# Moving the ada_w chunk loads of FFN1 from SyncE's DMA queue to GpSimd's

## What is computed

```python
m_lat = (jax.nn.silu(c) @ ada_w[l] + ada_b[l]).reshape(b, N_MOD, 1, d)
m_ctx = (jax.nn.silu(c_ctx)[None, :] @ ada_w[l] + ada_b[l]).reshape(1, N_MOD, 1, d)
x = x + 0.5 * m_lat[:, 2] * swiglu(modulate(rms_norm(x, norm1_g[l]), m_lat[:, 0], m_lat[:, 1]),
                                   ffn1_w_in[l], ffn1_w_out[l])
...
hx = modulate(rms_norm(x, norm2_g[l]), m_lat[:, 3], m_lat[:, 4])
```

## Time and profile before

| | us |
|---|---|
| median of 3 runs | 3235.8 |
| lowest and highest run | 3230.8 and 3244.4 |
| span of the profiled execution (first to last instruction) | 3242.2 |
| VectorE busy | 1721.2 |
| ScalarE busy | 945.0 |
| GpSimd busy | 4.5 |

### The profile page before, as it was taken

How to read it: one execution, slowest core, us unless ns; L and a number is a source line. 1 busy time by engine, 2 the same in 40 slices (tenths; PEclk the granted TensorE clock), 3 DMA queues, 4 the chain that set the end, 5 groups by cost and what they waited for, 6 DMA issues and landing times.

```text
span 3242.2 us, 40985 instructions
## 1 busy us (share of the span) xinstructions
PE 2930.8 (90%) x16213; PEld 2527.8 (78%) x16213; DVE 1721.2 (53%) x1907; ACT 945.0 (29%) x928; POOL 4.5 (0%) x13
## 2 busy tenths in 40 slices
PE   4659999999898989999999699977999999999997
PEld 3437787787777777778888598755688999999997
DVE  5765565656565555553342832265356555555555
ACT  4552121211111111212122532134234333333333
POOL 0000000000000000000000000000000000000000
PEclk9989999999999999999999899978898999999998
DMA  6755454544665665652333263312144666666662
GB/s 246 277 194 172 139 174 115 177 136 137 194 195 170 193 204 176 222 149 91 102 92 99 64 181 104 91 39 65 52 134 139 181 181 181 181 181 180 180 179 95
DMA packets 529879, 491.42 MB, mean 152 GB/s; under 512 B 17698, under 2 KB 448152, under 8 KB 523032
## 3 DMA queue, kind: packets, MB, share of 16 engines
q1 hardware_dynamic: 529464, 489.00, 49.5%
q0 software_dynamic: 352, 1.58, 0.2%
HBM read 488.44 MB, written 2.10 MB: 151 GB/s over the span
## 4 chain that ended last, share of the span: by engine, by line
PE 74%; DVE 9%; DMA 8%; ACT 5%; issue 4%; SPq 0%; DVEq 0%; ACTq 0%
PE py L736 9%; PE py L737 9%; PE py L738 9%; DMA chunk<-in_ada_w 7%; PE pg L736 6%; PE pg L737 6%; PE pg L738 6%; PE pu L736 6%; PE pu L737 6%; PE pu L738 6%; ACT wh L449 4%; DVE accl L1271 2%; DVE wl L1103 2%; PE py L885 1%; PE py L886 1%
## 5 line engine op out<-in xcount | busy, mean ns | idle before, releaser
L1103 DVE TENSOR_TENSOR wl<-raw,wh 128x2048 fp32r<-128x2048 f32 x364 | 833.8, 2291 | 828.6 <-ACT wh L449 828.4
L449 ACT ACTIVATE wh<-raw 128x2048 fp32r<-128x2048 f32 x364 | 695.4, 1911 | 1333.6 <-PE py L738 633.3
L736 PE MATMUL py<-ah,wh 128*128 128x512 f32 (+1 forms) x1408 | 481.4, 342 | 31.6 <-DVE xc L1232 26.3
L736 PE MATMUL pg<-hh,wh 128*128 128x512 f32 (+1 forms) x1408 | 478.8, 340 | 10.8 <-DVE hl L1167 6.3
L737 PE MATMUL py<-al,wh 128*128 128x512 f32 (+1 forms) x1408 | 477.3, 339 | 0.0
L738 PE MATMUL py<-ah,wl 128*128 128x512 f32 (+1 forms) x1408 | 476.7, 339 | 0.0
L736 PE MATMUL pu<-hh,wh 128*128 128x512 f32 (+1 forms) x1408 | 476.3, 338 | 0.0
L737 PE MATMUL pg<-hl,wh 128*128 128x512 f32 (+1 forms) x1408 | 476.1, 338 | 0.0
L738 PE MATMUL pg<-hh,wl 128*128 128x512 f32 (+1 forms) x1408 | 476.0, 338 | 0.0
L737 PE MATMUL pu<-hl,wh 128*128 128x512 f32 (+1 forms) x1408 | 475.5, 338 | 0.0
L738 PE MATMUL pu<-hh,wl 128*128 128x512 f32 (+1 forms) x1408 | 474.9, 337 | 0.0
(11 more groups left out here) (272 smaller groups left out, 2838.6 us busy)
## 6 DMA issues: line engine op xcount, KB each, us to landing
raw<-in_ffn_w_in SPq DMA_DIRECT2D x176, 1024.0 KB
chunk<-in_ada_w SPq DMA_DIRECT2D x192, 512.0 KB, 4.3
raw<-in_ffn_w_out SPq DMA_DIRECT2D x88, 1024.0 KB
raw<-in_ada_w SPq DMA_DIRECT2D x48, 1024.0 KB
raw<-in_mix_w_in SPq DMA_DIRECT2D x30, 1024.0 KB
raw<-in_mix_w_out SPq DMA_DIRECT2D x16, 1024.0 KB
raw<-in_mla_w_uq SPq DMA_DIRECT2D x12, 256.0 KB
xnat<-in_x SPq DMA_DIRECT2D x2, 1024.0 KB, 16.3
```

Source lines behind the costliest of these rows:

```text
L449: nc.scalar.activation(wh[:, slot % 2, :], raw[:, slot, :], ACT.Copy).then_inc(wh_ready, 1)
L736: mm(out_ap, w[0], xh_ap, start=first, stop=False, skip_group_check=True)
L1103: tt(wl[:, slot % 2, :], raw[:, slot, :], wh[:, slot % 2, :].bitcast(F32), ALU.subtract).then_inc(wl_ready, 1)
```

## The change

The 192 chunk loads are taken out of SyncE's loops. GpSimd gets them in two loops of its own, with the same wait on `chunk_free` and the same increment of `chunk_loaded`, so the order of the chunks and the two buffers are as before. They are issued as the loads of GpSimd's DMA queue (q0, which the profile calls software_dynamic; SyncE's is q1, hardware_dynamic). What the other engines do is the same, instruction for instruction.

```diff
--- before.py
+++ after.py
@@ -310,12 +310,6 @@
                     dst = raw[:, slot, :].rearrange("p (t n) -> p t n", n=512)
                 sp.dma_start(dst, src).then_inc(raw_loaded[slot], 64)
 
-            def chunk_load(unit, t, count):
-
-
-                sp.wait_ge(chunk_free, count + 1)
-                sp.dma_start(chunk[:, t % 2, :], ada_w[0, t * P:(t + 1) * P, ds(unit * CH + 3 * D, CH)]).then_inc(chunk_loaded[t % 2], 16)
-
             for s in range(RAW):
                 sp.wait_ge(wl_ready, FFN1_0 - RAW + s + 1)
                 ffn_slab(ffn1_w_in, ffn1_w_out, 0, s, s)
@@ -331,19 +325,9 @@
             with sp.Fori(0, 4) as i:
                 for s in range(GSLABS):
                     ahead(i, s)
-                    if s < 8:
-                        for t in (2 * s, 2 * s + 1):
-                            chunk_load(i, t, i * KT + t)
-
             with sp.Fori(4, 8) as i:
                 for s in range(GSLABS):
                     ahead(i, s)
-                    if s < 4:
-                        for t in range(4 * s, 4 * s + 4):
-                            chunk_load(i * 2 - 4, t, (i - 4) * (2 * KT) + t + 4 * KT)
-                    elif 5 <= s < 9:
-                        for t in range(4 * s - 20, 4 * s - 16):
-                            chunk_load(i * 2 - 3, t, (i - 4) * (2 * KT) + t + 5 * KT)
             for s in range(GSLABS - RAW):
                 ahead(8, s)
             with sp.Fori(9, GROUPS) as i:
@@ -422,6 +406,17 @@
             nc.gpsimd.memset(csp[:].bitcast(F32).rearrange("p a b -> p (a b)"), 0.0).then_inc(consts_ready, 1)
             for f, w in enumerate((ret_decay_fwd, ret_decay_bwd)):
                 pool.dma_start(dec[:, f * HEADS:(f + 1) * HEADS], w.to_broadcast([P, HEADS])).then_inc(rope_loaded, 16)
+
+            def chunk_load(unit, t, count):
+                pool.wait_ge(chunk_free, count + 1)
+                pool.dma_start(chunk[:, t % 2, :], ada_w[0, t * P:(t + 1) * P, ds(unit * CH + 3 * D, CH)]).then_inc(chunk_loaded[t % 2], 16)
+
+            with pool.Fori(0, 4) as i:
+                for t in range(KT):
+                    chunk_load(i, t, i * KT + t)
+            with pool.Fori(0, 8) as i:
+                for t in range(KT):
+                    chunk_load(i + 4, t, i * KT + (4 * KT + t))
 
             pool.wait_ge(y_free, Y_OUT)
             pool.dma_start(ropes[:].rearrange("p a b -> p (a b)"), rope).then_inc(rope_loaded, 16)
```

## The result

The changed kernel takes 3282.3 us (median of 4 runs, 3269.5 to 3285.0), the kernel before 3237.3 beside it: the ratio is 1.013, with a 95% interval from 1.0104 to 1.0155. It is 45 us slower. Forecast were 3207 us, within 3186 to 3262. All 192 chunk loads moved to GpSimd's queue.

What follows compares the result with a forecast made beforehand. It took chunk-load waits in groups 4 to 7 as the bound, about 51 us. Savings of 2.9, 2.3 and 2.0 (clock) made 7.2 us a group, 29 in four, off the median 3235.8: 3207 us, range 3186 to 3262.

Steps and rivals of the forecast that it cites:

- What bounds the kernel: FFN1 groups 4 to 7 lose some 12.7 us each to late chunk loads, about 51 us in all.
- VectorE's two kinds of round: Chunk loads in groups 4 to 7 took 3.58 us to landing, or 6.65 us when queued behind a slab load.
- TensorE's two waits: Per group in groups 4 to 7: 9.25 us ahead of the transposes at slab 5, 6.86 us ahead of slab 9.
- The price of a GpSimd load: Per chunk round, 0.22+0.15 us more than on SyncE, plus 0.1 us for a register address (bounds 0 and 0.3).
- d: Time the early slab load adds to the landing of c2: taken as 0.5 us, bounds 0.2 and 1.4.
- c2: Third of a step's four chunks, issued when the first one's operation ends; forecast to land after 3.8 us plus d.
- c4: First chunk of the next step, issued after c2's operation; its 6.65 us round was to become near 3.8.
- the working of the first half: Wait ahead of slab 5: 3.7+4d plus 0.7 us, so 6.4 us where it was 9.3; 2.9 won a group.
- the second half: Wait ahead of slab 9: 2.6+3d plus 0.5 us, so 4.6 us where it was 6.9; 2.3 won a group.
- The clock: Shorter TensorE stalls in groups 4 to 7 raise the granted clock: up to 3.4 us a group, 2.0 taken.
- Rival B: c2 waits for the slab's rest instead of c4: 3220 to 3240 us, chance 0.25.
- Rival C: GpSimd's loads are held up while VectorE works, at c2: 3250 to 3277 us, chance 0.23.

Runs made afterwards that it cites:

- experiment 5: Kernel before with four chunk buffers in groups 4 to 7, not two: 3160.5 us with loads on SyncE, 3159.5 us with loads on GpSimd and early slabs.
- experiment 2: Kernel before, chunks still on SyncE, but in groups 4 to 7 each slab load goes out early, ahead of the step's third chunk load: 3282.1 us, ratio 1.0153.
- e11: e5 with SyncE's slab loads in groups 4 to 7 held until GpSimd has issued the step's fourth chunk load: 3260.9 us, ratio 1.0057.
- experiment 1: Slab loads of groups 4 to 7 cut to one sixteenth in both kernels: 3239.2 us with chunks on GpSimd, 3223.4 us with them on SyncE.
- e5: Changed kernel with GpSimd's two loops unrolled, so every address and wait is a constant: 3275.9 us, ratio 1.0131.
- e7: Changed kernel, but in groups 4 to 7 SyncE issues a slab load only when the step's third chunk has landed: 3271.8 us, ratio 1.0127.
- e8: e7 with GpSimd's loops unrolled, so all its addresses and waits are constants: 3274.4 us, ratio 1.0113.

## Why the prediction was wrong

**What bounds the kernel** held: the loss of groups 4 to 7, VectorE's two kinds of round, TensorE's two waits. Groups 0 to 3 and the part behind group 7 didn't change, as said. Only the bound on what better chunk loads can win, 51 us, was too low: experiment 5 won some 73. The bound took the early groups' 139.8 us as the floor, and without waits a group of the second stretch takes 132.5.

**The price of a GpSimd load** was near. Landing alone 3.8 was taken, 3.9 measured. From release to issue 0.39 was taken (0.29 and 0.1 for a register address), 0.63 measured. With that corrected alone the forecast would still have been a gain.

**The step that failed is the slab's**, d, what a slab adds to the landing of c2. I took 0.5 us with an upper bound of 1.4. Measured in the first half of group 4, c2's kind of round took 6.1, 7.2, 5.2 and 6.2 us, so d is 2.3, 3.4, 1.4 and 2.4. The prediction had named the sign for this, a landing of c2 over 5.2 us. Two things were wrong in it. First, "the difference, 3.07 us, is what a slab costs the load behind it": the slab of the earlier trace rows had been issued 3.2 us ahead of c4, so 3.07 us were what was left of it, not the whole. A whole slab holds the DMA engines for about 4 us, and in the changed kernel it goes out 1.1 us ahead of c2, not 1.5. Second, the estimate from `dec`: a small load into a queue of its own landed long before SyncE's, and I took this to mean that the second queue is served beside the first. The rows above show little of that for a chunk: q0 got next to nothing until three quarters or more of the slab had been moved. The rule of the Trainium skill on turns between the queues (DMA: Bandwidth & Descriptors, Queues, rings and completion order), which I took to put d at the low bound, fits only the last part of it, the stretch from 849 to 852.5 in which both queues had engine time; d came out far above that bound either way. With one queue in order (experiment 2) c2 landed 7.4 us after its issue and 8.0 after the slab's; here it was 6.1 and 7.2.

**The waits around it were modelled well.** Put the four measured values into the working of the first half: 3.7 + 9.5 + 0.7 = 13.9 us for the wait ahead of slab 5. The profile has

```profile
884.20 1.11 PE L798 MATMUL pa<-eyes,accl 128*128 128x128 f32 x4 [13.95 <-DVE accl L1266]
```

That it fits to 0.1 us is in part luck: the loads also started 0.24 us later than the working has it, up to 1.7 us over seven rounds, which is not in this sum and which other terms must have made good (c3 came right behind c2, not 1.6 us behind it, and a start is hidden where VectorE is busy anyway). In the second half d was 1.6, 2.8 and 2.9, and the working gives 2.6 + 7.3 + 0.5 = 10.4 us. Measured were 7.3 ahead of slab 9 and 2.1 in a wait for the low part (L1240) that the working doesn't have.

**The clock** was to give back 2.0 us a group. Its granted value fell instead, from 0.94 to 0.91 in group 4, where the stalls grew. With the measured d and no clock the working loses 4.6 and 3.5 us a group, 3268 in all (an estimate); so these two make up 61 of the 75 us between 3207 and 3282.

**Rival B** had the mechanism (the slab's rest ahead of c2 and not of c4) with its price cut off at d = 1.4, which made it no change. That the same 4 us are cheap ahead of c4 and dear ahead of c2 stood in the formulas (the 3.5 us of VectorE's work before c4), and I didn't ask what moving the slab costs by itself: experiment 2 shows that it costs as much as the whole change, 47 us against 45. **Rival C** gave the right side for a wrong reason: with no slab in the way, GpSimd's load of c2 lands in 3.9 us while VectorE works. This case's runs don't show the trap of the Trainium skill (SBUF — State Buffer, SBUF: two separate sides) for these operations.

The two costs don't add up. In the stretch of 524.0 us, the slab early costs 31 us alone (experiment 2), GpSimd alone 17 (e11) or 19 (experiment 1), and together they cost 37; by the medians of the whole kernel it is 47, 20 or 16, and 45. A late start is hidden where a slab stands in front anyway. Left open is why the engines move most of the slab first when the chunk comes from another queue, what of GpSimd's cost is the late start and what is the queue, and whether a second hardware queue would be served otherwise; it wasn't tried.

## What to carry to other kernels

An issue list is also a timetable for the DMA engines. Before taking loads out of it, look at where the loads that stay will go: freed of the waits, they go out earlier, and with 1 MB each they are now ahead of the small load that someone waits for. Where a load is late because it may only be issued when a buffer comes free, try another buffer before another queue: here two more buffers of 512 KB won 2.2%, and made all of the differences between the queues disappear.

## What the runs showed of the hardware

- A load from GpSimd with its address and wait from registers starts 0.63 us after its release, with constants 0.3 (e5), from SyncE 0.17 with registers.
- 1 MB in rows of 512 bytes held the DMA engines about 4 us (832.6 to 836.5 in the changed kernel); the next two chunks, 1 MB in rows of 4 KB, about 3 (836 to 839).
- A load on the second queue got no engine time for 3 us while the load that was issued 1.1 us earlier on the first was being moved; with no slab in front the first packets came after 1.1 to 1.6 us. One step later both queues had engine time at once from 849 to 852.5, when three quarters of the slab had been moved.
- Behind c3 and a slab, c4 landed 9.3 to 9.8 us after the slab's issue in four kernels (before, e7, e8, e11), whether its own load was issued 1.5 or 3.3 us behind the slab.
